# Loading the weights of a 32-expert layer by chunk of a pair of experts instead of by expert

## What is computed

```python
    def expert_block(args):
        xe, e = args
        gu = xe @ w_gu[e] + b_gu[e]
        g, u = gu[:, :D_FF], gu[:, D_FF:]
        g = jnp.minimum(g, SWIGLU_LIMIT)
        u = jnp.clip(u, -SWIGLU_LIMIT, SWIGLU_LIMIT)
        h = (u + 1) * (g * jax.nn.sigmoid(SWIGLU_ALPHA * g))
        return h @ w_down[e] + b_down[e]
```

## Time and profile before

| | us |
|---|---|
| median of three runs | 1069.05 (1067.43 to 1069.20) |
| the profiled execution | 1069.07 |
| its span in the profile | 1067.2 |
| PE busy | 1020.8 |
| first part of the layer, until the first expert step | 155 |
| one pair of experts in the middle | 58.8 |

### The profile page before, as it was taken

How to read it: one execution, slowest core, us unless ns; L and a number is a source line. 1 busy time by engine, 2 the same in 40 slices (tenths; PEclk the granted TensorE clock), 3 DMA queues, 4 the chain that set the end, 5 groups by cost and what they waited for, 6 DMA issues and landing times.

```text
span 1067.2 us, 11841 instructions
## 1 busy us (share of the span) xinstructions
PE 1020.8 (96%) x5107; PEld 476.6 (45%) x5108; DVE 325.4 (30%) x579; ACT 91.9 (9%) x163; POOL 7.4 (1%) x19
## 2 busy tenths in 40 slices
PE   9999999999999999989898989989898989999997
PEld 7767354444444444434343434434343434334333
DVE  4633031143323232322323241323223232413243
ACT  2222020010000000000000010000000000100001
POOL 0100000000000000000000000000000000000000
PEclk9999999999999999999999999999999999999999
DMA  9960969999999999999999999999999999999996
GB/s 355 322 171 2 395 252 379 413 422 416 417 425 429 427 427 429 425 429 428 429 429 426 430 427 429 427 429 430 426 428 429 427 431 426 429 416 421 421 421 260
DMA packets 60597, 420.39 MB, mean 394 GB/s; under 512 B 21293, under 2 KB 21617, under 8 KB 28945
## 3 DMA queue, kind: packets, MB, share of 16 engines
q1 hardware_dynamic: 60096, 419.32, 95.2%
q0 software_dynamic: 352, 0.55, 0.2%
q10 hardware_dynamic: 112, 0.03, 0.0%
HBM read 418.29 MB, written 1.58 MB: 393 GB/s over the span
## 4 chain that ended last, share of the span: by engine, by line
PE 68%; DMA 30%; DVE 0%; issue 0%; SPq 0%; ACT 0%; DVEq 0%
PE ps L937 35%; DMA ring<-in_w_gu_dram 27%; PE ps L953 6%; PE ps L854 5%; PE ps L775 5%; PE ps L979 3%; DMA ring<-in_w_down_dram 3%; PE ps L793 3%; PE ps L646 2%; PE ps L865 2%; PE ps L939 1%; PE ps L964 1%; PE ps L981 1%; PE ps L804 1%; PE ps L1134 1%; PE ps L743 0%
## 5 line engine op out<-in xcount | busy, mean ns | idle before, releaser
L937 PE MATMUL ps<-ring,xT 128*64 128x512 f32 x1008 | 458.1, 608 | 28.4 <-DMA ring<-in_w_gu_dram 27.8
L939 PE MATMUL ps<-ring,xT 128*64 128x512 f32 x1000 | 455.4, 609 | 0.0
L937 PEld LDWEIGHTS ps<-ring,xT 128*64 128x64 f32 x1008 | 136.0, 139 | 303.8 <-issue 299.3
L953 PE MATMUL ps<-ring,he 128*64 128x512 f32 x472 | 210.5, 595 | 8.8 <-DMA ring<-in_w_down_dram 7.9
L955 PE MATMUL ps<-ring,he 128*64 128x512 f32 x472 | 211.0, 596 | 0.0
L939 PEld LDWEIGHTS ps<-ring,xT 128*64 128x64 f32 x1000 | 135.0, 140 | 0.0
L953 PEld LDWEIGHTS ps<-ring,he 128*64 128x64 f32 x472 | 61.8, 137 | 136.6 <-issue 136.4
L1756 DVE TENSOR_TENSOR acc<-ps,acc 128x512 f32<-128x512 f32 x52 | 33.7, 686 | 185.0 <-PE ps L979 185.0
L854 PE MATMUL ps<-oh,x 128*128 128x128 f32 x512 | 69.3, 287 | 0.0
L854 PEld LDWEIGHTS ps<-oh,x 128*128 128x128 f32 x512 | 64.6, 197 | 8.0 <-issue 5.1
L1370 ACT COPY gu_sb<-ps 128x1024 f32<-128x1024 f32 x16 | 16.2, 1012 | 579.2 <-PE ps L939 579.2
(11 more groups left out here) (269 smaller groups left out, 721.2 us busy)
## 6 DMA issues: line engine op xcount, KB each, us to landing
ring<-in_w_gu_dram SPq DMA_DIRECT2D x86, 2048.0 KB, 27.0
ring<-in_w_down_dram SPq DMA_DIRECT2D x46, 2048.0 KB, 27.1
ring<-in_w_gu_dram SPq DMA_DIRECT2D x79, 1024.0 KB, 12.4
ring<-in_w_down_dram SPq DMA_DIRECT2D x32, 1024.0 KB, 25.8
w_chc<-in_w_in_dram SPq DMA_DIRECT2D x1, 4096.0 KB, 20.1
w_qkv<-in_w_in_dram SPq DMA_DIRECT2D x4, 768.0 KB, 8.1
w_b<-in_w_in_dram SPq DMA_DIRECT2D x1, 2048.0 KB, 26.3
w_o<-in_w_out_dram SPq DMA_DIRECT2D x2, 1024.0 KB, 23.4
```

Of the source, the lines that this page charges most:

```text
L937: even = mm(gu_banks(j)[0:CAP, n, :], xT[j % 2][:, k, 0:CAP], first[n], start=(k == 0), stop=(k == KT - 1))
L939: odd = mm(gu_banks(j)[CAP:P, n, :], xT[j % 2][:, k, CAP:P], second[n], start=(k == 0), stop=(k == KT - 1))
L953: even = mm(out[0:CAP, half, :], hid[:, f, 0:CAP], first[2 * a + half], start=(f == 0), stop=(f == FT - 1))
```

## The change

From the 36th ring chunk on (`SINGLE` = 35 earlier ones stay as they were), a load takes chunk c of both experts of a pair to two neighbouring slots. Its source has two pieces of 8 KB per partition, one in each expert's matrix; its destination is 16 KB per partition in one piece. `ORDER` becomes the order of use throughout. Single loads remain where the first of the two would be slot 15, and where one chunk of a pair has its place elsewhere.

```diff
         EARLY, FINE = 2 * 2 * GUC + 2 * DNC, 4 * GUC + 4
-        ORDER[:EARLY] = IN_USE[:EARLY]
-        ORDER[ALL - FINE:] = IN_USE[ALL - FINE:]
+        ORDER = list(IN_USE)
...
         SINGLE = EARLY - 5
-        FIRST_TWO = SINGLE + 2 * (GUC + DNC + GUC)
         LOADS, n = [], 0
         while n < RINGED - 2:
-            e, c = ORDER[n]
-            two = (FIRST_TWO <= n < RINGED + 1 - FINE and c % 2 == 0 and ORDER[n + 1] == (e, c + 1)
-                   and slot_of(n) < RING - 1)
-            LOADS.append((n, 1 + two))
-            n += 1 + two
-
-        for n in range(SINGLE, FIRST_TWO, 4):
-            LOADS[n:n + 4] = sorted(LOADS[n:n + 4], key=lambda load: used_up_to(*ORDER[load[0] - RING]))
+            (e, c), after = ORDER[n], ORDER[n + 1]
+            of_both = slot_of(n) < RING - 1 and n >= SINGLE and e % 2 == 0 and after == (e + 1, c)
+            LOADS.append((n, 1 + of_both))
+            n += LOADS[-1][1]
...
+            def load_both(e, c, slot):
+                src = gu_dram[e:e + 2, c // 2] if c < GUC else dn_dram[e:e + 2, (c - GUC) // 2]
+                sp.dma_start(ring[:, slot:slot + 2, :],
+                             src[:, :, c % 2 * FLAT:(c % 2 + 1) * FLAT].rearrange("s p f -> p s f")
+                             ).then_inc(chunk_in[slot], 16)
+
             for first, many in LOADS[RING:]:
                 sp.wait_ge(chunk_used, max(used_up_to(*ORDER[n - RING]) for n in range(first, first + many)))
-                load(*ORDER[first], many, slot_of(first))
+                if many == 2 and ORDER[first + 1][0] != ORDER[first][0]:
+                    load_both(*ORDER[first], slot_of(first))
+                else:
+                    load(*ORDER[first], many, slot_of(first))
```

## The result

| | before | changed |
|---|---|---|
| median, us | 1068.29 (1067.43 to 1069.93, 6 runs) | 1078.26 (1077.14 to 1079.94, 6 runs) |
| ratio | | 1.0091, 95% interval 1.0081 to 1.0102 |
| profiled execution, us | 1069.07 | 1078.36 |

The change costs 10.0 us by the medians; 7.5 were forecast (1076.6, in a range of 1069 to 1083).

What follows compares the result with a forecast made beforehand. The prediction took the DMA stream to bound the kernel from about 165 us until the last loads. Packets at +8.4 us and ends at -0.9 us gave +7.5 us on 1069.07, so 1076.6 us, range 1069 to 1083.

Steps and rivals of the forecast that it cites:

- Step 1: Middle of the changed profile: 256 data packets of 8 KB a load, rate 423 GB/s, 59.5 us a pair.
- step 3: Changed profile: median time from a load's issue to landing above 27 us, DMA share still full.
- Step 2: Changed profile at 204 to 249 us and near the end: rate 423 GB/s in place of 421.
- Term (1): 132 loads of 16 KB rows become 8 KB rows, 1056 more packets an engine at 8 ns: +8.4 us.
- Term (2): Single loads become loads of two, 36 load ends fewer at 25 ns each: -0.9 us.
- Term (3): Loads wait for one PE step, half issued a step earlier; worth nothing because the queue was never empty.
- Term (4): PE's 2.7 us waits for loads become at most 1.5 us; a gain for PE, 0 for the stream.
- Term (5): Up to 7 loads queued, SP may hand one over more slowly, only further loads stand behind: 0.
- Rival A: In the DMA stream, cost lies in load ends or packets do not double: 1067 to 1071 us, chance 0.10.
- Rival B: In the DMA stream, packets cost nothing and fewer ends save 3.2 us: 1065.9 us, chance 0.05.
- Rival C: Memory reads alternating between two places 4 or 8 MB apart lose bandwidth: costs more than 14 us, chance 0.06.
- Rival D: PE becomes the bound if it slows after each wait, having about 6 us a pair; chance 0.01.

Runs made afterwards that it cites:

- e10: Changed kernel with loads of both experts only in the middle, where the kernel before loads two chunks of one expert: 1079.19 us, ratio 1.0095.
- e5: Changed kernel with loads of both experts only where the kernel before loads chunk by chunk, two of one expert in the middle: 1068.76 us, ratio 1.0007.
- e3: Changed kernel with each load of two chunks read in four pieces of 4 KB per partition instead of two of 8 KB: 1102.77 us, ratio 1.0322.
- e2: Kernel before with two neighbouring loads, one per expert, made into one 4 MB load in 16 KB pieces: 1069.13 us, ratio 1.0006.
- e6: Kernel before with all ring loads of 1 MB, one for each chunk: 1078.09 us, ratio 1.0084.
- e4: Changed kernel with each load from the 36th ring chunk on issued one PE step later: 1083.06 us, ratio 1.0142.
- e1: Kernel before with loads of two chunks of one expert sent to slots s and s+2, destination in two 8 KB pieces: 1077.99 us, ratio 1.0095.
- e8: Kernel before with gate and up in the middle loaded four chunks at a time, 32 KB per partition in one piece: 1100.69 us, ratio 1.0292.

## Why the prediction was right, point by point

**What bounds the kernel: right.** The DMA share is full in both, the middle's rate fell by 1.5% and the whole time by 0.9%, since only the middle had the faster rate. Step 1 of what the changed profile would show came out (256 packets a load, 421.9 GB/s for a forecast of 423, within 421 to 426), and step 3 did (33 us to landing). Step 2 didn't: at 204 to 249 us and near the end the rate stayed at 421, and 423 were expected from the ends saved. e10 and e5 place the loss.

**Term (1), the packets: right in kind, short in size.** +8.4 us were forecast, at 8 ns a packet; it is 9.6 ns and 10.1 us. The step that missed is the choice between the two early rows. w_b's row of 2 KB packets had given 9.7 ns (84.9 less 75.2), w_chc's row of 4 KB packets 7.2, and I went by the one nearer in packet size. The price turned out hardly to depend on the size: 9.6 from 16 to 8 KB and 9.4 from 8 to 4 KB (e3). The row with the most packets for its bytes, where the price is the largest part of what is measured, was the better witness. Why w_chc's row lies under the 9.4 ns of e3's packets of the same size stays open: in the twelve traces its 6 us have 414 to 419 GB/s, which gives 6 to 8 ns, and other small transfers stood beside it.

**Term (2), the ends: wrong in size.** -0.9 us were forecast, at 25 ns; it is about 0 (e5, e2), at most 2 to 3 ns an end (e6), or -0.1 us. The 25 ns were a remainder: 89 ns less eight packets. And the 89 itself came from comparing 421 GB/s in an early and a late stretch with 428 in the middle. Compared at the same place, one load of 16 KB rows against two of 8 KB rows is 4.974 - 4.894 = 80 ns (e6), of which 77 are packets. Both misses have one sign, and together they are the 2.5 us that the forecast lacks.

**Term (3), the earlier issue: right here, but not for the reason given.** I wrote that the queue was never empty. It wasn't in either kernel, from 200 us on, but between 205 and 270 us it nearly was: one step later costs 5 us (e4). The changed kernel's loads there land 12.7 us after their issue, the kernel before's 12.3, so it keeps what little queue there is, and this term is 0.

**Term (4), PE's shorter waits: right.** 1.2 to 1.4 us in the pair shown, below the 1.5 forecast; the products after them stood at 0.61. The mean clock rose to 0.997, worth nothing to the stream. One wait above the forecast's 1.6 us is left, of 2.27 us at 1026 us in the last pair.

**Term (5), more in flight: right.** 33 us from issue to landing in place of 27, a hand-over of 4 us on SP, and no cost: e1 has the same rate with a hand-over of 0.54 us.

**Rival A** (ends, or packets that do not double because the destination is one piece) fell to the packet row, 256 a load, and to the rate, 421.9 GB/s where a price of nil would have left 428. **Rival B** needed a packet below 0.9 ns (0.8 by its own sum), far under the 9.6 measured. **Rival C** (two places in memory) fell to e1, which is as slow with one place, and e2, which is as fast as before with two. The Trainium skill's rule on the row pitch, named there, is about the pitch from partition to partition, in copies between tensors in HBM; that pitch stayed here, so the rule doesn't reach this case. **Rival D** (PE slowed after each wait): its busy time fell.

## What to carry to other kernels

In a stream of loads that keeps the DMA engines full, count the data packets on each engine and multiply: their number is set by the shorter contiguous run of source and destination, and here it decided the sign of the change, while the number of loads did nothing. Where its queue is short such a stream can run dry although no engine waits, so look for the stretch with the shortest time from issue to landing before loads are made larger or later. And take a price from the row in which it is the largest share, and compare rates only at the same place of the program.

## What the runs showed of the hardware

- A data packet cost one DMA engine 9.4 to 9.6 ns beside its bytes, from 16 to 8 KB and from 8 to 4 KB (before, changed, e3). By an estimate from this, the bytes alone go at 2.0972/(4.894 - 0.077) = 435 GB/s, the figure that the Trainium skill gives as the ceiling ("DMA: Bandwidth & Descriptors", "Where 436 GB/s comes from"). Packets of 32 KB were seen (e8).
- The end of a load, with its 16 small packets, cost at most 2 to 3 ns an engine in a full queue (e6, e2). Of the 2 us a transfer that the Trainium skill gives ("DMA: Bandwidth & Descriptors", "Anatomy of one DMA", for transfers issued by GpSimd; these are issued by SP) no more than that is seen in such a stream.
- With about 7 loads of 17 packets an engine in flight (33 us to landing) SP took a median of 4 us to hand over the next, and with fewer 0.54 us (28 us to landing, e1). The rate was 422 GB/s in both. What limit lies between wasn't measured.
- Two matrices 4 or 8 MB apart, read in turn in one load, ran at the full rate in pieces of 16 KB (429 GB/s, e2).
